# Attention in a two-block transformer kernel: VectorE takes the unit's maximum first, then scales the older unit's probabilities

## The reference

```python
def _masked_softmax(logits, mask):
    return jax.nn.softmax(jnp.where(mask, logits, NEG), axis=-1)

# first block, twice: differential attention (two maps a head), latent attention, top-k attention
p = _masked_softmax(logits, _chunk_mask(qpos, kpos))
a = p[:, :, 0] - lam * p[:, :, 1]           # differential attention alone: two maps become one
o = jnp.einsum('bhqk,bkhd->bqhd', a, v)

# second block, layer 0: neighbourhood attention for latent tokens, full attention for context tokens
p = jax.nn.softmax(s, axis=-1)              # s: window logits + bias, and the context's logits
o = p_loc @ v_win + p_ctx @ v_ctx

# second block, layer 1: grouped-query attention, 256 latent queries over 512 keys
p = jax.nn.softmax(jnp.einsum('bqkgd,btkd->bkgqt', q, k), axis=-1)
o = jnp.einsum('bkgqt,btkd->bqkgd', p, v)
```

## Time and profile before

| | us |
|---|---|
| median of 3 runs | 1828.99 (1827.28 to 1829.86) |
| the profiled execution, device time | 1828.82 |
| the profiled execution, span of its trace | 1827.2 |
| TensorE matmul busy | 1571.9 (86%) |
| TensorE weight load busy | 1122.2 (61%) |
| VectorE busy | 550.9 (30%) |
| ScalarE busy | 340.5 (19%) |
| GpSimd busy | 86.8 (5%) |
| TensorE's granted clock, mean | 0.92 of full |

### The profile page before, as it was taken

One profiled execution on the slowest core, in us unless ns is written; L12 is line 12 of the kernel. 1 busy time (PEld: TensorE's weight loads), 2 busy tenths in 40 slices (PEclk: granted clock), 3 DMA queues, 4 the chain that ended last, 5 costly groups with the idle time before them and its releaser, 6 DMA issues.

```text
span 1827.2 us, 27494 instructions
## 1 busy us (share of the span) xinstructions
PE 1571.9 (86%) x11350; PEld 1122.2 (61%) x11350; DVE 550.9 (30%) x1368; ACT 340.5 (19%) x744; POOL 86.8 (5%) x135
## 2 busy tenths in 40 slices
PE   7999899998879999999795999999379887787772
PEld 5787578885623856745334888988256565444441
DVE  2602613216244156115515111111155722000101
ACT  1311301114132033125103000000131321000000
POOL 0001000010100000000101000000100001000000
PEclk9899888998979899989997999999689998898996
DMA  7368423575632244210812999999452017999993
GB/s 245 98 177 261 132 73 84 162 229 168 173 114 74 90 150 153 69 46 1 281 48 93 375 389 396 396 393 368 156 184 69 24 46 287 400 395 393 400 403 129
DMA packets 183595, 371.18 MB, mean 203 GB/s; under 512 B 19412, under 2 KB 138032, under 8 KB 167008
## 3 DMA queue, kind: packets, MB, share of 16 engines
q1 hardware_dynamic: 164352, 322.90, 49.5%
q0 software_dynamic: 10560, 32.73, 5.7%
q10 hardware_dynamic: 8608, 14.51, 2.2%
HBM read 345.52 MB, written 24.59 MB: 203 GB/s over the span
## 4 chain that ended last, share of the span: by engine, by line
PE 63%; DMA 22%; DVE 8%; ACT 3%; issue 2%; SPq 1%; ACTq 0%; POOL 0%; POOLq 0%; DVEq 0%
PE ps_proj L572 28%; DMA ring<-in_exp_w 20%; PE ps_outp L572 13%; PE ps_outp L1172 9%; PE ps_score L572 4%; PE ps_proj L698 2%; PE ps_turn L725 2%; DVE probs L1816 1%; SPq L2497 1%; DVE rstd L1795 1%; PE ps_proj L1172 1%; PE ps_turn L572 1%; PE ps_proj L630 1%; PE ps_score L1172 1%; DVE h_t L2012 1%
## 5 line engine op out<-in xcount | busy, mean ns | idle before, releaser
L572 PE MATMUL ps_proj<-h_t,ring 128*128 128x256 f32 (+1 forms) x1280 | 360.8, 443 | 16.1 <-ACT h_t L1512 8.1
L572 PEld LDWEIGHTS ps_proj<-h_t,ring 128*128 128x128 f32 x1280 | 252.5, 199 | 122.3 <-issue 86.4
L1172 PE MATMUL ps_outp<-ring,arena 128*32 128x384 f32 (+3 forms) x1792 | 164.3, 440 | 61.0 <-DMA ring<-in_exp_w 60.2
L1172 PEld LDWEIGHTS ps_outp<-ring,arena 128*32 128x32 f32 (+1 forms) x1792 | 113.4, 128 | 102.7 <-issue 79.9
L1172 PE MATMUL ps_score<-ring,arena 128*32 128x384 f32 (+2 forms) x2048 | 148.8, 381 | 16.7 <-DMA ring<-in_exp_w 16.5
L1172 PE MATMUL ps_proj<-ring,arena 128*32 128x128 f32 (+2 forms) x2048 | 150.5, 384 | 7.9 <-DMA ring<-in_exp_w 5.1
L1172 PEld LDWEIGHTS ps_proj<-ring,arena 128*32 128x32 f32 (+1 forms) x2048 | 124.5, 118 | 31.6 <-DMA ring<-in_exp_w 9.0
L1172 PEld LDWEIGHTS ps_score<-ring,arena 128*32 128x32 f32 (+1 forms) x2048 | 117.3, 116 | 42.8 <-DMA ring<-in_exp_w 25.3
L2258 DVE COPY arena<-ps_score 128x384 f32<-128x384 f32 (+1 forms) x32 | 15.7, 491 | 329.7 <-PE ps_score L1201 329.7
L572 PE MATMUL ps_proj<-ring,h_t 128*128 128x256 f32 (+1 forms) x512 | 106.4, 366 | 0.4 <-ACT arena L1536 0.4
L572 PEld LDWEIGHTS ps_proj<-ring,h_t 128*128 128x128 f32 x512 | 93.0, 192 | 14.6 <-issue 3.2
(11 more groups left out here) (284 smaller groups left out, 1578.6 us busy)
## 6 DMA issues: line engine op xcount, KB each, us to landing
ring<-in_exp_w SPq DMA_DIRECT2D x192, 1024.0 KB, 11.3
ring<-in_ada_w SPq DMA_DIRECT2D x48, 1024.0 KB, 6.3
ring<-in_w_in SPq DMA_DIRECT2D x30, 1024.0 KB, 5.9
ring<-in_even_w_in SPq DMA_DIRECT2D x12, 1024.0 KB, 5.7
ring<-in_w_out SPq DMA_DIRECT2D x8, 1024.0 KB, 6.2
expert_in<-arena POOLq DMA_DIRECT2D x1, 6144.0 KB, 27.7
ring<-in_odd_w_in SPq DMA_DIRECT2D x6, 1024.0 KB, 11.5
arena<-expert_in POOLq DMA_DIRECT2D x15, 384.0 KB, 8.3
```

The costliest lines, as they stand in the source:

```text
L572: last = pe.matmul(out, w, a, start=(i == 0), stop=(i == len(pairs) - 1))
L1172: last = pe.matmul(b[p0:p0 + pn, c0:c0 + wn], x_of(p0, lo, pn), w[:, w0:w0 + wn], start=first and p0 not in strip[:i], stop=done and p0 no ...
```

## The change

In the loop of VectorE's `attention` the block that waits for unit i-1's exponentials and scales its probabilities moves behind the block that takes unit i's maximum. It still stands ahead of the copy of unit i-1's transposes. Nothing is added and nothing is removed; TensorE's and ScalarE's streams are as they were.

```diff
                 for i in range(n + 2):
-                    if 1 <= i <= n:
-                        regions, maps, nk, _, scale, _ = units[i - 1]
-                        u = base + i - 1
-                        par = u % 2
-                        pr = probs[:, par, :]
-                        dve.wait_ge(drained["score"], mark["score", u])
-                        nr = 2 * maps if maps == 2 else len(regions)
-                        step(dve.reciprocal(inv[:, par, 0:nr], total[:, par, 0:nr]))
...
-                        ins.then_inc(probs_scaled, 1)
                     if i < n:
                         regions, maps = units[i][0:2]
...
                             ins.then_inc(max_ready, 1)
                             mark["score", base + i] = use["score"]
                     if 1 <= i <= n:
+                        regions, maps, nk, _, scale, _ = units[i - 1]
+                        u = base + i - 1
+                        par = u % 2
+                        pr = probs[:, par, :]
+                        dve.wait_ge(drained["score"], mark["score", u])
+                        nr = 2 * maps if maps == 2 else len(regions)
+                        step(dve.reciprocal(inv[:, par, 0:nr], total[:, par, 0:nr]))
+                        if maps == 2:
+                            step(dve.tensor_scalar(inv[:, par, 2:4], inv[:, par, 2:4], scale, None, ALU.mult))
+                        for r, (lo, hi) in enumerate(regions):
+                            ins = dve.tensor_scalar(pr[:, lo:hi], pr[:, lo:hi], inv[:, par, r:r + 1], None, ALU.mult)
+                            if maps == 2:
+                                step(ins)
+                                ins = dve.scalar_tensor_tensor(out=pr[:, lo:hi], in0=probs_m[:, par, lo:hi],
+                                                               scalar=inv[:, par, 2 + r:3 + r], in1=pr[:, lo:hi],
+                                                               op0=ALU.mult, op1=ALU.add)
+                        ins.then_inc(probs_scaled, 1)
                         turn_copy(probs_t[:, (base + i - 1) % 2, 0:nk * P], nk * P)
```

## The result

The changed kernel takes 1972.19 us (median of 4 runs, 1970.28 to 1974.5) against 1828.13 (median of 4): 1.0793 times the time before, 95% interval 1.0769 to 1.0816. That is slower by 144 us, where 80 were forecast and 1948 was the end of the range.

A forecast was written before the change was run, and what follows sets the result against it. TensorE itself was taken as the bound in most of the attention. Added gaps of 31.8 us (first block), 31.6 and 17.1 us (second block's layers 0 and 1) sum to 80.5 on 1828.8: 1909 us, range 1894 to 1948.

The forecast's parts named there:

- closed chain: In each attention step: scores(i), maximum(i), scaling(i-1), transposes(i-1), values(i-2), scores(i+1), with TensorE only waiting ahead of the transposes.
- direct cost: Longer gaps from scores to transposes in the four attentions, without any clock change: 31.8, 31.6 and 17.1 us, sum 80.5.
- the terms of the latent and the top-k steps: First block, per layer: latent steps 5 to 7 cost 4.5 us more, top-k steps 8 to 11 cost 4.2 us.
- The clock: TensorE's granted clock in the attentions: 0 us in the sum for a fall to half, though new gaps leave TensorE idle.
- the possible 92 us: Cost of half clock: 49 us in second block's layer 0, 28 in its layer 1, some 15 in first block.
- two-map steps: First block, differential units, steps 1 to 4 of each layer: +1.6, +0.9, +2.0 and +2.7, sum 7.2 us a layer.
- the clock rival: TensorE's clock falls in the attentions' new gaps: half of the possible 92 us on top, about 1955 us; chance 0.18.
- differential stretch: First block, where the granted clock went from 1.00 to 0.50 before the change; TensorE's share of work before the fall 0.61.
- step 4: First block: a latent unit's scores with a differential unit's scaling, gap 4.78 us against 2.08, so +2.7 us.
- Faster: Rival: the softmax loop was the bound, early exponentials remove TensorE's 19.8 us wait ahead of the transposes: 1809 us; chance 0.03.
- No change: Rival: the attentions' added gaps are swallowed downstream or VectorE's part hides, within 0.2% of 1829 us; chance 0.03.

## Why the prediction was wrong

*Direction, order and place were right.* That "each step gets a closed chain" is what the timeline and the kernel with earlier scores show.

*The sum of the direct cost was right in the second block* (31.8 and 17.1 measured at full clock, 31.6 and 17.1 forecast), gap by gap: 2.52 to 2.75 us in layer 0, 2.40 in layer 1. So were the terms of the latent and the top-k steps, 4.5 and 4.2 us. The idle of VectorE hid nothing, and nothing was given back downstream (-1.2 us in the rest of the span).

*The step that failed is "The clock": "I take 0 in the sum", and half of the possible 92 us as the upper part of the range.* Against the kernel before, the profiled span grew by 141.5 us, 61 more than the sum of 80.5: 40.8 of them in the second block's layer 0, 21.4 in the first block's calls, 0 in layer 1 of the second block. In the calls where the excess is, the clock was 0.65 to 0.69, and it goes when the clock is held. So, but for the 2.4 us by which the two-map steps were mis-sized (below), the 0 had to be 61, two thirds of the 92. Half was too little: the rival's 1955 is 17 us under the result, and the range ended at 1948, even below that. The prediction named a clock below 1.00 in the second block as a sign that the clock rival holds, and the sign came.

The reason that I gave, a share of work near 0.7 above the 0.61 of the differential stretch, does not decide: the second block's layer 0 fell in its second step, in a stretch in which TensorE was busy 2.61 of 4 us, while layer 1 stayed at 1.00, busy 38.98 of 61.17 us. The per-call sizes in the forecast were good for layer 0 of the second block (49 us for a clock that stays down; 40.6 measured, as it came back for some steps during or behind each modulation block), too low for the first block (15 for its latent and top-k steps; 29.3 between the clock as it was and a clock of 1.00 throughout, in both layers), and wrong for layer 1 (28; 0).

The Trainium skill, "TensorE: Matmul & The Clock Gate", section "A second HAM failure mode: psum-queue depth-cycling", describes a kernel whose clock swings between the two levels because of frequent short idles between groups of matmuls. The trace after agrees in three of the four calls (mean clock 0.69, 0.65, 0.65) and not in the last, which has gaps of 2.40 us every 3.79 us and stays at 1.00.

*Two smaller terms.* In the differential steps both maxima, 1.2 us, stand ahead of the scaling, not the second alone. The profile after, step 2 (against the earlier trace rows):
```profile
178.89 0.90 PE L725 MATMUL ps_turn<-const,probs 128*128 128x128 f32 x3 [2.62 <-DVE probs L1841]
179.72 1.66 PE L572 MATMUL ps_score<-arena 32*128 32x128 f32 x8
...
181.41 0.30 DVE L1819 CUSTOM_DVE_ANT_0 ps_score<-ps_score,arena 128x128 f32<-128x128 f32 x1 [1.02 <-PE ps_score L572]
...
182.64 0.17 DVE L1834 RECIPROCAL inv<-total 128x4 f32<-128x4 f32 x1
...
184.62 0.90 PE L725 MATMUL ps_turn<-const,probs 128*128 128x128 f32 x3 [3.24 <-DVE probs L1841]
```
The first maximum starts at 181.41, when both maps' scores are done, and the reciprocal 1.23 us later; from transposes to transposes it is 5.7 us, where 5.4 were forecast. With the new order in these steps alone they cost 8.2 us in layer 0 and 8.6 in layer 1, where 7.2 were forecast. And I costed step 4 and the latent steps at full clock, as they had been, without asking what state the slower steps ahead of them would hand over. The kernel with two-map steps alone shows that this costs 7.0 and 6.8 us in steps that the order does not touch.

*The rivals.* "Faster" had for it ScalarE's 64.2 us of waits; they became 126.7 us while the kernel got slower, as the maxima now wait for TensorE's later scores. "No change" needed cover downstream; there was none (-1.2 us). "The clock falls in the new gaps" is what happened, in three calls of four, and with more than the half that it was given.

## What to carry to other kernels

In an in-order engine that serves two stages of a pipeline, put first what the bounding engine waits for next; work on the newer unit placed ahead of it ties the bounding engine's next step to its own last output. When a change opens regular idle time on TensorE, work out the time at both clock levels and carry the level into the stages behind it, also those that the change does not touch. A cheap test of which part is clock is to fill the idle time with matmuls into a bank that is about to be overwritten; if that makes the kernel faster, useful work or an earlier issue of the next unit belongs there. Here they gave 43 and 89 us back, and the idle-time matmuls 78; none of them reached the kernel before, whose order had no such gaps.

## What the runs showed of the hardware

- In the second block's layer 0 a hand-over that is late by some 1.45 us a step cost 31.8 us at full clock and 72.4 us where the clock fell.
- The clock did not come back as soon as TensorE was busy again. Behind the two-map steps it was 0.59 on the mean of 18.95 us without an idle moment: 0.50 for the first 14.4 us (206.10 to 220.48), and 1.00 from within the modulation block that followed.
- Of two calls with nearly the same gap (2.57 and 2.40 us) and the same number of transposes, the one with products of 64 rows or columns fell to half the clock and the one with 128 x 128 products kept 1.00 throughout, at a busy share of 38.98 of 61.17 us. With the scores issued earlier, and gaps of 1.05 to 2.02 us, the first kept 1.00 too. What separates the two calls was not tested.
- Matmuls that compute nothing of use can pay: in the changed kernel the filled gaps saved 77.5 us of the span, in the kernel before some 4 us (0.2%).
